# Weight tiles stored in pairs with their columns in turn, and weight slots moved by 64 bytes, in a two-layer fp32 diffusion backbone

## What is computed

```
def conv_ffn(u, w_up, conv_w, conv_b, w_down):
    a, g = jnp.split(u @ w_up, 2, axis=-1)
    ...
    return (jax.nn.gelu(a) * g) @ w_down
...
    for layer in range(DEPTH):
        ...
        h = h + g1 * y.astype(h.dtype)
        u = rms_norm(h, norm_ffn_w[layer]) * (1.0 + sc2) + sh2
        h = h + g2 * conv_ffn(u, ffn_w_up[layer], ffn_conv_w[layer], ffn_conv_b[layer], ffn_w_down[layer])
```

## Time and profile before

| | |
|---|---|
| median of 3 runs | 1783.16 us (1775.05 to 1783.86) |
| profiled execution | 1782.06 us, of which 1780.2 us from the first to the last instruction |
| PE, matmuls busy | 1709.4 us, 96% |
| PEld, weight loads busy | 1484.1 us, 83% |
| DVE / ACT / POOL busy | 52% / 42% / 31% |
| TensorE clock granted | 0.984 of 2.4 GHz in the mean |

### The profile page before, as it was taken

The page is one execution under the profiler, slowest core; times in us unless marked ns, Lnnn a source line. Parts: engine busy times, 40 slices in busy tenths (PEclk is TensorE's granted clock), DMA queues, the critical chain, the costliest instruction groups (busy, mean ns, idle before and its releaser), DMA issues.

```text
span 1780.2 us, 26540 instructions
## 1 busy us (share of the span) xinstructions
PE 1709.4 (96%) x9744; PEld 1484.1 (83%) x9744; DVE 924.7 (52%) x1468; ACT 755.4 (42%) x1208; POOL 543.3 (31%) x249
## 2 busy tenths in 40 slices
PE   5999899997999999999999999999999899999997
PEld 2777788896899999999988888997668888888876
DVE  5777966667956566566523365001774532222344
ACT  3563434776332332323333445212884443334442
POOL 1122113553222332233222323322004234444442
PEclk9999999998999999999999999999999999999998
DMA  8323223443432433433321122121322123222221
GB/s 335 138 95 119 73 72 100 138 132 130 142 119 96 141 130 107 142 121 116 100 67 60 60 72 84 60 95 59 105 74 83 60 82 96 95 95 96 94 95 59
DMA packets 66588, 184.08 MB, mean 103 GB/s; under 512 B 5920, under 2 KB 26784, under 8 KB 65200
## 3 DMA queue, kind: packets, MB, share of 16 engines
q1 hardware_dynamic: 44784, 164.69, 27.4%
q10 hardware_dynamic: 21696, 17.88, 3.4%
HBM read 180.40 MB, written 2.15 MB: 103 GB/s over the span
## 4 chain that ended last, share of the span: by engine, by line
PE 80%; DVE 5%; ACT 2%; issue 1%; POOL 0%; ACTq 0%; DVEq 0%; POOLq 0%
PE ps L2363 28%; PE ps L2789 13%; PE ps L2362 13%; PE ps L2376 4%; PE ps L2443 3%; PE ps L2786 3%; PE ps L2721 2%; PE ps L2923 2%; PE ps L2902 2%; PE ps L2936 2%; PE ps L2449 1%; PE ps L2346 1%; PE ps L2456 1%; PE ps L2345 1%; PE ps L2636 1%
## 5 line engine op out<-in xcount | busy, mean ns | idle before, releaser
L692 POOL TENSOR_TENSOR wsp<-raw,wsp 128x1024 fp32r<-128x1024 f32 x185 | 457.0, 2470 | 1133.5 <-ACT wsp L763 1133.1
L763 ACT ACTIVATE wsp<-raw 128x1024 fp32r<-128x1024 f32 x185 | 196.3, 1061 | 453.1 <-PE ps L2363 350.5
L2362 PE MATMUL ps<-v_a,wsp 128*128 128x384 f32 x1008 | 342.7, 340 | 0.0
L2363 PE MATMUL ps<-v_b,wsp 128*128 128x386 f32 x1008 | 340.2, 337 | 0.0
L2789 PE MATMUL ps<-hsp,wsp 128*128 128x512 f32 x984 | 277.4, 393 | 2.5 <-DVE hsp L2009 2.5
L2789 PEld LDWEIGHTS ps<-hsp,wsp 128*128 128x128 f32 x984 | 183.6, 188 | 45.3 <-issue 4.4
L2363 PE MATMUL ps<-uf,wsp 128*128 128x512 f32 x888 | 201.4, 389 | 0.0
L2363 PEld LDWEIGHTS ps<-uf,wsp 128*128 128x128 f32 x888 | 166.7, 188 | 34.6
L2363 PEld LDWEIGHTS ps<-v_b,wsp 128*128 128x128 f32 x1008 | 193.5, 192 | 0.0
L2362 PEld LDWEIGHTS ps<-v_a,wsp 128*128 128x128 f32 x1008 | 189.2, 188 | 0.0
L2026 DVE SCALAR_TENSOR_TENSOR conv<-apad,vec,conv 128x770 f32<-128x770 f32 (+1 forms) x44 | 47.6, 1082 | 204.2 <-ACT conv L1201 204.2
(11 more groups left out here) (320 smaller groups left out, 2537.2 us busy)
## 6 DMA issues: line engine op xcount, KB each, us to landing
raw<-in_weights SPq DMA_DIRECT2D x281, 512.0 KB, 3.8
nab<-in_nabias ACTq DMA_DIRECT2D x32, 256.0 KB, 3.0
start_w<-in_start SPq DMA_DIRECT2D x6, 1024.0 KB, 20.9
h<-in_x SPq DMA_DIRECT2D x4, 768.0 KB, 14.5
mD<-rows_scratch ACTq DMA_DIRECT2D x12, 256.0 KB, 4.1
mqs<-rows_scratch ACTq DMA_DIRECT2D x12, 256.0 KB, 5.3
h<-in_x ACTq DMA_DIRECT2D x2, 1536.0 KB, 6.4
start_w<-in_start SPq DMA_DIRECT2D x4, 512.0 KB, 12.5
```

The source lines that it names most:

```text
L692: pool.tensor_tensor(w[:, 1, :], raw[:, raw_index(s) % 4, :], w[:, 0, :].bitcast(F32), ALU.subtract)\
L763: act.activation(split_of(s)[:, 0, :], raw[:, raw_s % 4, :], ACT.Copy).then_inc(*own.one(hi_ready))
L2362: pe.matmul(cx, w, x_cx[:, k, xp, :], start=first, stop=last)
L2363: mm = pe.matmul(lat, w, x_lat[:, k, xp, :], start=first, stop=last)
```

## The change

The host stores each pair of neighbouring weight tiles with their columns in turn: column 0 of the one, column 0 of the other, column 1 of the one, and so on (`in_pairs`). A tile is then read with a step of two elements: its 128 columns stand 8 bytes apart over 1024 bytes of the row, where they stood 4 bytes apart over 512 bytes. Every matmul that has a weight tile as stationary operand gets it by `weights_of`. The blocks that `tokens` uses as moving operand stay as they were.

The slots `wsp`, `w_wide` and `w_wide1` begin 64 bytes later than before, which puts each tile 64 bytes (or 68, for the second of a pair) behind the place that the operands have modulo 256. The small buffers behind `wsp` (`ident`, `vec` and so on) move by 64 bytes with it, and the large area behind them by 256. `hsp` lies 256 bytes lower within its area, and so at the address it had.

No instruction is added, removed or put in another order on any engine, and no transfer changes its size.

```
 BLOCK = 1024
+LINE_STEP = 64
...
         raw = take("raw", [P, RAW_SLOTS, BLOCK])
+        place[0] += LINE_STEP
         wsp = take("wsp", [P, SPLIT_SLOTS, 2, BLOCK], F32R)
...
-        w_wide1 = at("w_wide1", [P, WIDE_SLOTS, 2, BLOCK], ar + 32768, F32R)
-        assert ar + 32768 + WIDE_SLOTS * 8192 <= f0
+        w_wide1 = at("w_wide1", [P, WIDE_SLOTS, 2, BLOCK], ar + 32768 + LINE_STEP, F32R)
+        assert ar + 32768 + 256 + WIDE_SLOTS * 8192 <= f0
...
-        w_wide = at("w_wide", [P, WIDE_SLOTS, 2, BLOCK], v_off, F32R)
-        hcx = at("hcx", [P, 2 * N_LATE, 2, N_CTX], v_off + WIDE_SLOTS * 8192, F32R)
+        w_wide = at("w_wide", [P, WIDE_SLOTS, 2, BLOCK], v_off + LINE_STEP, F32R)
+        hcx = at("hcx", [P, 2 * N_LATE, 2, N_CTX], v_off + WIDE_SLOTS * 8192 + 256, F32R)
...
-        hsp = at("hsp", [P, 2, 2, N_TOK], f0 + 18944, F32R)
+        hsp = at("hsp", [P, 2, 2, N_TOK], f0 + 18688, F32R)
...
+        def weights_of(s, wp, k):
+
+            pair = split_of(s)[:, wp, 2 * P * (k // 2):2 * P * (k // 2) + 2 * P]
+            return pair.rearrange("p (c t) -> p c t", t=2)[:, :, k % 2]
...
-                        w = split_of(s)[:, wp, tile(k)]
+                        w = weights_of(s, wp, k)
...
-                        w = split_of(s_down + b)[:, wp, 512 * kk + P * mm_:512 * kk + P * mm_ + P]
+                        w = weights_of(s_down + b, wp, 4 * kk + mm_)
...
-    return w.reshape(KT, P, m, P).transpose(2, 1, 0, 3).reshape(m, P, BLOCK)
+    return in_pairs(w.reshape(KT, P, m, P).transpose(2, 1, 0, 3).reshape(m, P, BLOCK))
+
+
+def in_pairs(blocks):
+
+    n = blocks.shape[0]
+    return blocks.reshape(n, P, KT // 2, 2, P).transpose(0, 1, 2, 4, 3).reshape(n, P, BLOCK)
...
-    stream += [up(g["ffn_w_up"][0]), row_blocks(g["ffn_w_down"][0])]
+    stream += [up(g["ffn_w_up"][0]), in_pairs(row_blocks(g["ffn_w_down"][0]))]
```

More of the change, by code:

```diff
@@ L316, in build @@
         uf = at("uf", [P, KT, 2, N_LAT], ar, F32R)
-        w_wide1 = at("w_wide1", [P, WIDE_SLOTS, 2, BLOCK], ar + 32768, F32R)
-        assert ar + 32768 + WIDE_SLOTS * 8192 <= f0
+        w_wide1 = at("w_wide1", [P, WIDE_SLOTS, 2, BLOCK], ar + 32768 + LINE_STEP, F32R)
+        assert ar + 32768 + 256 + WIDE_SLOTS * 8192 <= f0
         rt_row = hid0b[:, FT - 1 - u_rows, :]
-        w_wide = at("w_wide", [P, WIDE_SLOTS, 2, BLOCK], v_off, F32R)
-        hcx = at("hcx", [P, 2 * N_LATE, 2, N_CTX], v_off + WIDE_SLOTS * 8192, F32R)
-        assert v_off + WIDE_SLOTS * 8192 + 2 * N_LATE * 2048 <= f0
+        w_wide = at("w_wide", [P, WIDE_SLOTS, 2, BLOCK], v_off + LINE_STEP, F32R)
+        hcx = at("hcx", [P, 2 * N_LATE, 2, N_CTX], v_off + WIDE_SLOTS * 8192 + 256, F32R)
+        assert v_off + WIDE_SLOTS * 8192 + 256 + 2 * N_LATE * 2048 <= f0
         apad = at("apad", [P, 2, PADW], f0)
@@ L325, in build @@
         gel = at("gel", [P, 2, CW], f0 + 12352)
-        hsp = at("hsp", [P, 2, 2, N_TOK], f0 + 18944, F32R)
-        assert f0 + 18944 + 4 * T <= AR_END
+        hsp = at("hsp", [P, 2, 2, N_TOK], f0 + 18688, F32R)
+        assert f0 + 18688 + 4 * T <= AR_END
         naq = at("naq", [P, KT, N_LAT], ar)
@@ L2342, in two_blocks @@
                         for a, (wp, xp) in enumerate(PASSES):
-                            w, first, last = split_of(s + b)[:, wp, tile(k)], k == 0 and a == 0, k == KT - 1 and a == 2
+                            w, first, last = weights_of(s + b, wp, k), k == 0 and a == 0, k == KT - 1 and a == 2
                             if cx is not None:
@@ L2442, in project @@
                     first, last = k == 0 and a == 0, k == KT - 1 and a == 2
-                    mm = pe.matmul(ps[:, n % 2, :], wsp[:, s % 2, wp, tile(k)], u[:, k, xp, LAT], start=first, stop=last,
+                    mm = pe.matmul(ps[:, n % 2, :], weights_of(s, wp, k), u[:, k, xp, LAT], start=first, stop=last,
                                    skip_group_check=True)
@@ L2448, in project @@
                             pe.wait_ge(cx_took.sem, n)
-                        mm = pe.matmul(ps[:, 2, 0:N_CTX], wsp[:, s % 2, wp, tile(c)], u[:, c, xp, CTX],
+                        mm = pe.matmul(ps[:, 2, 0:N_CTX], weights_of(s, wp, c), u[:, c, xp, CTX],
                                        start=(c == 0 and a == 0), stop=False, skip_group_check=True)
@@ L2455, in project @@
                         for a, (wp, xp) in enumerate(PASSES):
-                            mm = pe.matmul(ps[:, 2, 0:N_CTX], wsp[:, s % 2, wp, tile(c)], u[:, c, xp, CTX], start=False,
+                            mm = pe.matmul(ps[:, 2, 0:N_CTX], weights_of(s, wp, c), u[:, c, xp, CTX], start=False,
                                            stop=(c == KT - 1 and a == 2), skip_group_check=True)
@@ L2655, in out_first @@
                     for a, (wp, xp) in enumerate(PASSES):
-                        w = wsp[:, s % 2, wp, tile(k)]
+                        w = weights_of(s, wp, k)
                         first, last = k == 0 and a == 0, k == KT - 1 and a == 2
@@ L2720, in half_product @@
                 for a, (wp, xp) in enumerate(PASSES):
-                    mm = pe.matmul(out, split_of(s)[:, wp, tile(k)], x[:, k, xp, in_lat(t)], start=(k == 0 and a == 0),
+                    mm = pe.matmul(out, weights_of(s, wp, k), x[:, k, xp, in_lat(t)], start=(k == 0 and a == 0),
                                    stop=(k == KT - 1 and a == 2), skip_group_check=True)
@@ L2845, in late_context @@
                             for wp, xp in PASSES:
-                                mm = pe.matmul(ctx_of(mm_), split_of(s_down + b)[:, wp, 512 * kk + P * mm_:512 * kk + P * mm_ + P],
+                                mm = pe.matmul(ctx_of(mm_), weights_of(s_down + b, wp, 4 * kk + mm_),
                                                hcx[:, 2 * (b - FT + N_LATE) + kk, xp, :], start=False,
@@ L2947, in out_last @@
                     for a, (wp, xp) in enumerate(PASSES):
-                        mm = pe.matmul(ps[:, m, :], wsp[:, s % 2, wp, tile(k)], uy[:, k, xp, :], start=(k == 0 and a == 0),
+                        mm = pe.matmul(ps[:, m, :], weights_of(s, wp, k), uy[:, k, xp, :], start=(k == 0 and a == 0),
                                        stop=(k == KT - 1 and a == 2), skip_group_check=True)
@@ L3077 @@
     qkv = g["na_w_qkv"][0]
-    stream += [up(g["ffn_w_up"][0]), row_blocks(g["ffn_w_down"][0])]
+    stream += [up(g["ffn_w_up"][0]), in_pairs(row_blocks(g["ffn_w_down"][0]))]
     stream += [column_blocks(qkv[:, :2 * D]), row_blocks(qkv[:, 2 * D:]), column_blocks(g["na_w_out"][0])]
-    stream += [up(g["ffn_w_up"][1]), row_blocks(g["ffn_w_down"][1])]
+    stream += [up(g["ffn_w_up"][1]), in_pairs(row_blocks(g["ffn_w_down"][1]))]
     stream = np.concatenate(stream, axis=0)
```

## The result

The changed kernel takes 1789.72 us (median of 14 runs, 1788.32 to 1792.12) against 1784.48 for the kernel before (14 runs, 1775.05 to 1789.46): ratio 1.0038, interval 1.0022 to 1.0054. Forecast were 1720 us and a range up to 1815. The profiled execution took 1790.33 us, 1788.5 of it from first to last instruction, with a granted clock of 0.981.

The account below looks back on a forecast made before the run. PE's matmul distances were taken to bound the kernel; 75 us of excess removed, less 13 us for meetings left, leaves 62 us off 1782.06, so 1720 us, range 1697 to 1815.

Parts of the forecast that it names:

- What bounds the kernel: In most stages time is the number of matmuls times their distance; PE is busy 96% of the span.
- The excess of 13 to 20 ns: Every fp32r matmul takes 13 to 20 ns more than its columns need at one column per clock, 2.4 GHz.
- What the excess can be: The fp32r moving stream runs through the weight load's place twice per load; equal speed and 64 bytes would keep them apart.
- The sum: Gains over some 6,400 matmuls reading weight tiles, if each keeps only 2.5 ns over its columns: together 75 us.
- The load: Weight loads with a step of 8 bytes keep their length, 188 ns; twice the length, held unlikely, would give about 1980 us.
- `tokens`: Its moving slots lie 64 bytes off weights `u`: worst cost 3.5 us, full cure gains 6.5, taken as nothing.
- The rival that the excess isn't contention: Something else in the change of weights at 2.4 GHz makes the excess; no change, 1783 us, chance 0.13.
- The rival of counted fetches: Each line a load fetches delays the moving stream: excess doubles, 1857 us (0.14), or milder, up to 1815 (0.10); chance 0.24.

Follow-up runs that it names:

- the pairs alone: The change without its 64 bytes (LINE_STEP = 0): tiles in pairs, slots at the operands' place modulo 256 bytes; 1796.78 us, ratio 1.0063 to the kernel before.

## Why the prediction was wrong

- **What bounds the kernel** was right: PE's distances set the time, and a change of 3 to 6 ns in them shows in the span.
- **The excess of 13 to 20 ns** was measured rightly. The step that failed is "What the excess can be": that it consists of the moving stream running through the load's place twice per load. For 512 columns it is as large with two columns loaded (231.7 ns), and at none of the places tried did it fall under 13 ns. The excess of 512 columns has two parts: some 13 ns that every one of these matmuls pays, and 0 to 12 ns on top that vary, with the places among other things (up to 17.17 us / 72 = 238.5 ns in the changed kernel's down-projection of layer 0). The change acts on the second alone. For 256 columns the first part isn't fixed: it went from 13.3 ns down to 7.0 with 64 columns loaded, so there the load has a share.
- The evidence was read one way where it allowed two. Plain fp32 at 2 ns and the low clock at 0 show only that the excess goes with fp32r read at 9.6 bytes/ns. I took the equal speed of load and stream as the reason. The loads of two columns show that 512 fp32r columns pay without any such meeting; bf16 at full clock pays 2.5 ns. Both fit the stream's own rate as the reason, and a property of fp32r at full clock as well: no run separates the two.
- **The sum** of 75 us priced each term as if all excess could go. Measured: the up-projection of layer 0 gained 2070 x 1.1 = 2.3 us instead of 27.7; its down-projection, from 353.3 to 351.1 ns a pair, 250 x 2.2 = 0.6 instead of 6.8; layer 1's up-projection lost 3.1 instead of gaining 10.2; its down-projection lost 1.8 on the 288 matmuls of its longest row; 384 columns on `u` lost 384 x 3.7 = 1.4; `half_product` stayed at 120 ns instead of gaining 4.1 us. Two slips in the working changed nothing: 75 us and another 2.5 ns on each of 6,400 matmuls below 1782 is 1691, not 1697, and a block of the up-projection has some 47 matmuls in 8.3 us (2070 / 44 by the earlier trace rows), not 24 in 4.2.
- **The load** with a step of 8 bytes kept its length within 7 ns: that step was right.
- **`tokens`**, taken at nothing within -6.5 and +3.5 us, went from 227.1 to 229.1 ns: +1.2 us.
- The rival that the excess isn't contention (0.13) was the nearest: the time came out within 0.5%. Its reason was right for the larger part of the excess of 512 columns. What I held against it, 233.1 beside 228.1 for one form, belongs to the smaller part. The rival of counted fetches falls too: 64 fetches a load instead of 32 didn't double the excess, and fewer didn't lower it for 512 columns. The Trainium skill (SBUF — State Buffer, Who interferes with whom) says that PE never waits on anyone. In the small programs no other engine works beside it, so they don't test that; they show that the places of TensorE's own two operands count, since the place of the weights moves fp32r matmuls from 226.9 to 233.1 ns. The bf16 rows show nothing of the kind.

**Open:** what the 13 ns are inside the engine; why 384 with 386 columns keeps 350.9 ns in the kernel where the same order by itself took 346.3 with the same shift modulo 256; and why the down-projection behind it went from 353.3 to 346.7 ns a pair with its own operands unmoved. That the kernel's places differ modulo more than 256 bytes is a possibility, and wasn't tried.

## What to carry to other kernels

An excess that vanishes in two other cases names what those cases share, not the mechanism: before building on it, take away the suspected partner alone (here a load of two columns). Measure a place by itself in the kernel's own order of matmuls before moving buffers; such a program gave the kernel's long rows to 0.5 ns in most cases, and missed in three: 233.3 against 235.6 ns for the pairs alone, and the two cases left open above. And price only the part of a cost that is seen to vary between rows of one form (512 columns stood 226.7 to 233.1 ns apart in the earlier trace rows), not all that lies above the ideal.

## What the runs showed of the hardware

- fp32r with 512 columns at 2.4 GHz: never under 226.7 ns in these runs, with 2 to 128 columns loaded, with groups of one matmul or of 24 in PSUM, and at the eight places of the weights. bf16: 215.8 to 216.0 ns at three places. Plain fp32: 2.7 ns over its columns.
- fp32r with 256 columns: 120.0 ns with 128 columns loaded, 113.7 with 64, 115.4 with 2.
- 504, 510 and 512 columns of fp32r take the same time, 226.7 to 226.9 ns.
- Two moving operands of 256 and 512 columns in turn take 353.3 ns a pair with both at the same place modulo 256 bytes and 343.3 with the second 64 bytes later. In the kernel the first order also ran at 346.7 ns.
- Weight loads with columns 4, 8, 16 and 32 bytes apart: 188, 193, 309 and 330 ns. Moving columns 8 bytes apart: 452.9 ns for 512, twice the time.
